# Output tiles of the last norm: shift vector filled into the outputs early, tiles added by GpSimd's indirect transfers

## What is computed

```
x = layer_norm(alpha * x + moe(x), ln2_g, ln2_b)

def layer_norm(x, g, b):
    mu = x.mean(-1); var = ((x - mu) ** 2).mean(-1)
    return (x - mu) * rsqrt(var + eps) * g + b
```

## Time and profile before

| | us |
|---|---|
| median of 3 runs (1344.98 to 1349.28) | 1348.16 |
| the profiled execution | 1353.49 |
| span of its profile | 1351.70 |
| of it, from the last scatter's issue to the end | 31.2 (1320.50 to 1351.70) |

### The profile page before, as it was taken

The page is one execution under the profiler, slowest core; times in us unless marked ns, Lnnn a source line. Parts: engine busy times, 40 slices in busy tenths (PEclk is TensorE's granted clock), DMA queues, the critical chain, the costliest instruction groups (busy, mean ns, idle before and its releaser), DMA issues.

```text
span 1351.7 us, 34179 instructions
## 1 busy us (share of the span) xinstructions
PE 1183.2 (88%) x12540; PEld 523.4 (39%) x12541; DVE 515.8 (38%) x875; ACT 272.8 (20%) x533; POOL 244.5 (18%) x214
## 2 busy tenths in 40 slices
PE   7998999937899999998899989989898989999760
PEld 6886545512233333432233423332333332533210
DVE  2996637764232222232223232420423320432226
ACT  0003233410102230141121211130121211131213
POOL 4000001331111221142120311221121212120113
PEclk9998899958999999999999999999999999999765
DMA  9702831549999999999999999999999999999963
GB/s 358 199 3 85 295 152 34 231 147 410 415 419 412 409 413 410 417 391 414 417 410 415 410 412 413 383 406 416 416 408 414 410 419 371 390 406 419 412 218 129
DMA packets 79977, 463.19 MB, mean 343 GB/s; under 512 B 12324, under 2 KB 20873, under 8 KB 29709
## 3 DMA queue, kind: packets, MB, share of 16 engines
q1 hardware_dynamic: 69083, 438.76, 80.2%
q0 software_dynamic: 8768, 17.47, 5.1%
q10 hardware_dynamic: 2066, 6.32, 1.2%
HBM read 447.51 MB, written 19.48 MB: 345 GB/s over the span
## 4 chain that ended last, share of the span: by engine, by line
PE 51%; DMA 22%; issue 3%; DVE 2%; ACT 0%; SPq 0%; DVEq 0%; ACTq 0%; POOLq 0%; POOL 0%
PE pu L1865 32%; PE rest L1879 17%; DMA ring<-in_e_in 13%; DMA ring<-in_e_out 8%; PE pu L1859 1%; PE rest L1890 1%; DVE fin L2081 0%; DVE bn L2063 0%; DVE xgT L2002 0%; DVE mv L2074 0%; DMA fin<-acc_rows 0%; DMA acc_rows<-y,row 0%; PE rest L1884 0%; SPq L281 0%; DMA xq<-x_rows,idx 0%
## 5 line engine op out<-in xcount | busy, mean ns | idle before, releaser
L1865 PE MATMUL pu<-ring,xgT 128*32 128x512 f32 x5248 | 587.9, 601 | 35.9 <-DMA ring<-in_e_in 35.2
L1865 PEld LDWEIGHTS pu<-ring,xgT 128*32 128x32 f32 x5248 | 161.8, 111 | 444.1 <-issue 443.3
L1879 PE MATMUL rest<-ring,hid 128*32 128x256 f32 x5248 | 302.2, 388 | 23.8 <-DMA ring<-in_e_out 16.3
L2032 DVE TENSOR_SCALAR gg<-pu 128x1280 f32<-128x1280 f32 x32 | 47.7, 1492 | 604.6 <-PE pu L1865 604.6
L1789 POOL DMA_INDIRECT acc_rows<-y,row x82 | 110.7, 1350 | 747.7 <-ACT y L1945 731.5
L1879 PEld LDWEIGHTS rest<-ring,hid 128*32 128x32 f32 x5248 | 168.7, 112 | 147.6 <-issue 46.1
L1945 ACT ACTIVATE y<-rest,gate 32x256 f32 x328 | 152.8, 466 | 297.1 <-issue 293.4
L1925 ACT ACTIVATE ss<-gg 128x1280 f32<-128x1280 f32 x32 | 40.7, 1272 | 537.7 <-DVE gg L2032 537.7
L866 PE MATMUL pair<-xt,ring 128*128 128x260 f32 x448 | 101.2, 388 | 7.3 <-DMA ring<-in_w_in 5.6
L1779 POOL DMA_INDIRECT xq<-x_rows,idx x82 | 88.2, 1075 | 91.9 <-issue 80.0
L866 PEld LDWEIGHTS pair<-xt,ring 128*128 128x128 f32 x448 | 86.2, 193 | 21.2 <-DMA xt<-in_xT 7.4
(11 more groups left out here) (270 smaller groups left out, 547.7 us busy)
## 6 DMA issues: line engine op xcount, KB each, us to landing
ring<-in_e_in SPq DMA_DIRECT2D x256, 1024.0 KB, 24.2
ring<-in_e_out SPq DMA_DIRECT2D x128, 1024.0 KB, 25.5
ring<-in_w_in SPq DMA_DIRECT2D x3, 1536.0 KB, 24.7
ring<-in_w_in SPq DMA_DIRECT2D x5, 512.0 KB, 11.0
ring<-in_w_o SPq DMA_DIRECT2D x1, 2048.0 KB, 12.0
conv<-in_x_prompt SPq DMA_DIRECT2D x1, 2048.0 KB, 13.8
x_rows<-conv ACTq DMA_DIRECT2D x4, 512.0 KB
acc_rows<-conv ACTq DMA_DIRECT2D x4, 512.0 KB
```

The costliest lines, as they stand in the source:

```text
L1865: mm = nc.tensor.matmul(pu[quarter(c), j], xgT[:, j, k], w[:, :, c * QC:(c + 1) * QC], start=False, stop=k == KT - 1, skip_group_check=True)
L1879: mm = nc.tensor.matmul(py[quarter(c), j], hid[:, j, 2 * q + f], w[:, f, c * QC:(c + 1) * QC], start=False, stop=q == FT // 2 - 1 and f == ...
L2032: V.tensor_scalar(gg[:, :, :], pu[:, :, 0], SW_LIMIT, None, ALU.min).then_inc(g_ready, 1)
```

## The change

- Early in `first_block`, behind the bias split, POOL waits for `bias_rows` and issues five plain transfers that fill `y_prompt` (4 x 512 KB) and `y_sample` (32 KB) with `ln2_b`, DRAM to DRAM (semaphore `y_begun`).
- SP's load of `l2b` and the buffer are gone.
- DVE writes the 128 row numbers of each prompt tile into `out_rows` (four 128x1 operations) after the last job.
- The additions of `l2b` (four on POOL, one on DVE) and SP's five stores are gone. Instead POOL issues, for each tile as soon as it is scaled, one indirect transfer that adds the tile's rows to the rows of the output that `out_rows` names, and waits for all of them at the end.

```
@@ first_block, POOL @@
+            gp.wait_ge(bias_rows, 2 + 16 * 6 * NQ)
+            shift_row = o["ln2_b"].partition_broadcast(P)
+            for i in range(NT):
+                gp.dma_start(o["y_prompt"][0, i * P:(i + 1) * P], shift_row).then_inc(y_begun, 16)
+            gp.dma_start(o["y_sample"][:, 0], o["ln2_b"].partition_broadcast(NS)).then_inc(y_begun, 16)
             gp.wait_ge(conv_out, 1)
             nc.gpsimd.memset(ps48[:, :, :, :], 0.0).then_inc(probs_zero, 1)
@@ moe_block, SP @@
             sp.dma_start(l2g[:, :], o["ln2_g"].partition_broadcast(P)).then_inc(ln2_in, 16)
-            sp.dma_start(l2b[:, :], o["ln2_b"].partition_broadcast(P)).then_inc(ln2_in, 16)
...
             for i in LAST_TILES:
                 load_sums(sp, i)
-            for n, i in enumerate(LAST_TILES):
-                if n < NT:
-                    sp.wait_ge(y_ready, n + 1)
-                else:
-                    sp.wait_ge(last_ready, 1)
-                dst = o["y_prompt"][0, i * P:(i + 1) * P] if i < NT else o["y_sample"][:, 0]
-                sp.dma_start(dst, fin[0:rows(i), i]).then_inc(y_out, 16)
-            sp.wait_ge(y_out, 16 * (NT + 1))
@@ moe_block, POOL @@
-            for n, i in enumerate(LAST_TILES[:-1]):
+            gp.sem_inc(gathers, 1)
+            gp.wait_ge(y_begun, 16 * (NT + 1))
+            gp.wait_ge(out_named, NT)
+            for n, i in enumerate(LAST_TILES):
                 m = rows(i)
+                dst = o["y_prompt"][0] if i < NT else o["y_sample"][:, 0]
                 gp.wait_ge(scaled2, n + 1)
-                nc.gpsimd.tensor_tensor(fin[0:m, i], fin[0:m, i], l2b[0:m], ALU.add).then_inc(y_ready, 1)
+                nc.gpsimd.indirect_dma_start(
+                    out=dst, out_offset=bass.IndirectOffsetOnAxis(ap=out_rows[0:m, i % NT:i % NT + 1], axis=0),
+                    in_=fin[0:m, i], in_offset=None, compute_op=ALU.add,
+                    bounds_check=(SEQ if i < NT else NS) - 1, oob_is_err=False).then_inc(y_out, 16)
+            gp.wait_ge(y_out, 16 * (NT + 1))
@@ moe_block, DVE @@
             fc = Chain(d, sem("ln2_chain"))
-            d.wait_ge(ln2_in, 32)
+            for i in range(NT):
+                V.tensor_scalar(out_rows[:, i:i + 1], C("job"), float(i * P), None, ALU.add).then_inc(out_named, 1)
+            d.wait_ge(ln2_in, 16)
...
-            i = LAST_TILES[NT]
-            d.wait_ge(scaled2, NT + 1)
-            V.tensor_tensor(fin[0:rows(i), i], fin[0:rows(i), i], l2b[0:rows(i)], ALU.add).then_inc(last_ready, 1)
```

More of the change, by code:

```diff
@@ L275, in layer @@
         lists_in = sem("lists_in")
+        y_begun = sem("y_begun")
         more_lists_in = sem("more_lists_in")
@@ L293, in first_block @@
         o[k] for k in "ring lists lists_in more_lists_in jobs count brow drow C load_unit".split())
+    y_begun = o["y_begun"]
     x1_dram, acc_dram, lists_dram, q_dram = o["x1_dram"], o["acc_dram"], o["lists_dram"], o["q_dram"]
@@ L1641, in moe_block @@
 def moe_block(nc, o):
-    ring, lists, lists_in, more_lists_in, brow, drow, jobs, count, C, sem, load_unit, unit_in = (
-        o[k] for k in "ring lists lists_in more_lists_in brow drow jobs count C sem load_unit unit_in".split())
+    ring, lists, lists_in, more_lists_in, brow, drow, jobs, count, C, sem, load_unit, unit_in, y_begun = (
+        o[k] for k in "ring lists lists_in more_lists_in brow drow jobs count C sem load_unit unit_in y_begun".split())
     x1_dram, acc_dram = o["x1_dram"], o["acc_dram"]
@@ L1667, in moe_block @@
         l2g = sb("l2g", [P, D])
-        l2b = sb("l2b", [P, D])
+        out_rows = sb("out_rows", [P, NT], I32)
         fin = sb("fin", [P, NT + 1, D])
@@ L1703, in moe_block @@
         rstd2 = bsem("ln2_rstd_ready")
-        y_ready = bsem("y_ready")
-        last_ready = bsem("last_tile_ready")
+        out_named = bsem("out_rows_named")
         y_out = bsem("y_out")
```

## The result

| | before | after |
|---|---|---|
| median of 20 runs each, us | 1349.52 | 1353.20 |
| lowest to highest | 1344.98 to 1351.61 | 1348.36 to 1356.96 |
| the profiled execution | 1353.49 | 1351.78 |
| its span | 1351.70 | 1350.00 |
| start to the first gather's issue | 290.88 | 286.96 |

What follows compares the result with a forecast made beforehand. It took full DMA engines to bound the loop and DVE's chain, stalled by POOL's additions, the tail. Tail -0.9 and load -1.3 made -2.2 us, taking the median from 1348.16 to 1346.0, range 1342.0 to 1351.0.

Steps and rivals of the forecast that it cites:

- The stalls, 5.5 us: Second norm after the loop: four DVE operations stand still during POOL's additions, 5.5 us in all, gone without them.
- The issue, 1.45 us: POOL's queue in the tail: issuing one adding indirect transfer of 128 rows takes 1.45 us.
- rivals of 2.8 us and of 5.4 us: POOL's issue grows with rows above its floor (2.8 us, 1348.4, chance 0.17) or wholly by row (5.4 us, 1357.9, 0.12).
- The second issue held by DVE: Second prompt tile's issue on POOL waits for DVE's third scaling, starts in effect at 1340.5 and ends at 1341.8.
- the rival built on it: Second issue on POOL isn't held by DVE: span ends 1.9 us earlier, median 1345.0; chance 0.10.
- The transfers, 0.33 us per packet: Tail's DMA engines: an adding 4 KB packet takes 0.33 us, a tile 2.6 us, transfers running one behind the other.
- plain speed and an unhindered issue: Aside on the tail: packets at plain speed and an issue not held up would end the span 4 us earlier.
- 0.4 us for what follows the landing: End of the program: from the last transfer's landing to the span's end 0.4 us, as before the change.
- The load, 1.3 us: Job loop: dropping the 512 KB load of the shift vector saves 1.3 us of full DMA engines.
- hidden anyway: Rival in the loop: the shift vector's load cost nothing, only the tail's 0.9 us are left, 1347.3; chance 0.12.
- The fills, nothing: Early in POOL's queue, before 70 us: five fill issues of about 1 us each cost nothing, in idle time.
- The slower rival: POOL's queue behind the first prompt tile: the issue is paid by the row, 5.4 us, giving 1357.9; chance 0.12.

## Why the prediction was wrong

It gave the tail 0.9 us less, and the tail became 4.5 us longer: 5.4 us amiss. The loop it had right in sign and about in size. By its own steps:

- **The stalls, 5.5 us: right.** L2081 is at 0.15 to 0.16 us and L2088 near 1.22 in all tiles; the last scaling ends 21.2 us after the last scatter's issue, where the forecast's 1341.9 is 21.4. The kernel with all additions on DVE shows the same without any transfer of POOL.
- **The issue, 1.45 us: right in kind, 0.09 us too low.** It is 1.54. The rivals of 2.8 us and of 5.4 us fall: 8 rows take 1.32 us, 128 take 1.54. The addition itself makes an issue 0.5 us dearer (1.03 without it); this fits the scatters of 32 rows, dearer than a gather of 128 in the earlier trace rows.
- **The second issue held by DVE: right.** It takes 2.03 us where its neighbours take 1.54 to 1.57, and ends 1.4 us behind the end of DVE's scaling, 1335.54 after 1334.13; without addition the same issue is held too, 1.45 against 1.03. The trace of before has more of it than the one gather of the forecast: eight gathers and list scatters begin inside an operation of over 1 us on DVE with both inputs in SBUF, the memory beside the engines, and all eight end 0.85 to 0.93 us behind it (the one at 262.01 takes 1.95 us instead of 0.97). Three begin inside an addition with one input in PSUM, the memory that matmuls write to, and take 0.89 to 1.01 us as ever. What the Trainium skill infers ("SBUF — State Buffer", section "Who interferes with whom"), that a tensor_tensor and the generating of descriptors don't meet, does not hold for these issues, and the rival built on it falls. One size was off: an issue that waits for nothing else starts 0.8 us behind its scaled tile (1329.70 to 1330.50), not 0.3.
- **The transfers, 0.33 us per packet: right where the engines run full, too short around it.** 198 GB/s are 0.33 us per packet. But the first microsecond of the second tile moved 86 GB/s, 0.6 us lost, and the last engines straggled for about 1 us. With the later start, 0.2 us, the landing came 31.7 us after the last scatter's issue, not 29.9: 1.8 us of the 5.4. The slow start repeats in the other kernels with five adding transfers, the straggling varies; the kernel with SP's wait landed at 30.6. One aside of the forecast is mis-summed: plain speed and an unhindered issue give 4.9 us by its own terms, not 4; the low end of its range, 1342.0, goes with 4.9.
- **"0.4 us for what follows the landing": this step failed.** It took the 0.4 us from the end of the kernel before, where SP was the last to wait. The prediction's own part on the change had seen that the wait now stood on POOL, and then kept SP's price. POOL's drain makes it 4.0 us: 3.6 of the 5.4. The view of the last line in the trace of before has it: POOL's drain ended 3.2 us behind its last addition (1349.5 after 1346.30), hidden there, and its cover went with the wait. Both experiments on the wait's place bear this out, +3.1 us in the tail of the old kernel, and 3.05 us back in the changed one, 2.0 of them between landing and end.
- **The load, 1.3 us: about right.** By four of them 1.2 us each in the loops of the profiles, 0.9 by the ratios. The rival "hidden anyway" falls.
- **The fills, nothing: right.** Their issues are even half as long as estimated, 0.52 us.

The slower rival had the right sign for the wrong reason: it looked for the cost in POOL's issues, and it lay behind them, in the end of POOL's program. The sum with what was measured is 4.5 - 1.2 = 3.3 us, or 3.6 with 0.9 for the load; the medians say 3.7. The rest is within what these runs can tell.

Even with the wait on SP the change gains nothing that can be told (1.0006). POOL's drain still takes 1.6 us there (2.0 us between landing and end, against 0.4 in before). The rest of DVE's freed 5.5 us goes to four transfers that queue behind each other at half speed, in a place where nothing but their landing is left to wait for. With the sample rows and one prompt tile in this manner instead of all five, early enough to be done before the last store, and with both vectors loaded behind the loop, the gain is 0.4%; the late loads alone, with all additions on DVE, can't be told from no change (0.9993).

## What to carry to other kernels

When a change moves the last wait of a program to another engine, look up that engine's closing drain in the trace and put it into the sum; here the same wait cost 3.1 us more on GpSimd than on SyncE, whose drain is 0.01 to 0.14 us. Look at the engine's own queue as well: with transfers of its own still under way its drain ended behind them even where another engine waited. Transfers that add ran at half the speed of plain ones here, so they suit the tiles that are done early, and the last tile should leave by a plain store. Loads that are needed only behind a loop whose DMA engines are full belong behind that loop: about 1 us for each 512 KB here.

## What the runs showed of the hardware that was not expected

- GpSimd's drain at the end of its program takes 3.17 us even when GpSimd has been idle, and 3.58 in the kernels in which it issues the last transfers and waits for them. Where SP waits instead, it ended 1.8 us behind the landing of GpSimd's own transfers (one kernel, 10.88 us from its start). Why it lasts so long no run here shows.
- An indirect issue that adds costs 0.5 us more than one that overwrites, and its rows are nearly free: 1.32 us for 8, 1.54 for 128.
- Plain issues on GpSimd's queue take 0.52 us for 128 rows of 4 KB, half of an indirect one.
- A fresh stretch of adding transfers begins slowly: 86 GB/s in its first microsecond, with the engines' share at 1.14, and 198 GB/s after it. The plain rows have no such start: 410 GB/s at a share of 1.00 in the first full half microsecond.
- An indirect issue that begins while DVE runs an operation with both inputs in SBUF ended 0.85 to 0.93 us behind that operation (eight of eight in the trace of before), and 1.4 us behind it when the issue adds; beside an operation with one input in PSUM it was not held (three issues, 0.89 to 1.01 us).
